# Index logits in pairs of heads, tie operations spread over the attention items, score banks that alternate

## What is computed

```python
# indexer and selected attention (dsa_attention), per block of 128 queries
logits = einsum('bqhd,bsd->bqhs', iq, ik) * 64**-0.5          # 8 index heads, one shared key
score = einsum('bqhs,bqh->bqs', relu(logits), iw * 8**-0.5)
score = where(key_chunk <= query_chunk, score, -inf)
_, idx = top_k(score, 256)                                     # equal scores: the lowest index wins
s = q . k[idx] * 64**-0.5 + t5_table[bucket(idx - qpos)]
out = softmax(s) @ v[idx]
...
# chunk_band_attention: each chunk of 64 sees itself and 8 chunks before it, plus a relative bias
# memory_attention: softmax(q . km * 64**-0.5) @ vm over 256 memory tokens
mixed = concat([ya * silu(a_g), yb * silu(bg), yc * silu(cg), ym * silu(mg)])
y = mixed @ w_out + b_out
```

## Time and profile before

| | |
|---|---|
| three runs | 3225.81, 3226.44, 3231.88 us |
| profiled execution | 3226.48 us, span 3224.7 us |
| busy in the span | PE 2913.3 us (90%), DVE 1745.2 (54%), ACT 874.9 (27%), POOL 634.5 (20%) |
| index logits (TensorE's first to last) | 1204.8 to 1284.7 us |
| remaining rows and channels, counting | to 1557.5 us on PE, 1539.8 on DVE |
| ties | 1540.0 to 1576.7 us |
| attention items | 1561.7 to 1761.8 us |

### The profile page before, as it was taken

One profiled execution on the slowest core, in us unless ns is written; L12 is line 12 of the kernel. 1 busy time (PEld: TensorE's weight loads), 2 busy tenths in 40 slices (PEclk: granted clock), 3 DMA queues, 4 the chain that ended last, 5 costly groups with the idle time before them and its releaser, 6 DMA issues. The chain is left out here.

```text
span 3224.7 us, 34616 instructions
## 1 busy us (share of the span) xinstructions
PE 2913.3 (90%) x13624; PEld 2334.2 (72%) x13624; DVE 1745.2 (54%) x2465; ACT 874.9 (27%) x1262; POOL 634.5 (20%) x298
## 2 busy tenths in 40 slices
PE   6899999999999899999687989955688999998997
PEld 3788888788887684888455768845576888886876
DVE  3699997737256705939767624068763322322032
ACT  2111112234143315121365201134421212222221
POOL 0000000001000010022000024436302434333664
PEclk9999999999999999999799989978898999999999
DMA  6111322233355410111101221100031111112343
GB/s 245 59 53 59 100 77 72 91 123 109 111 163 151 150 48 20 51 46 46 43 1 52 106 69 52 39 0 0 27 122 61 46 52 46 52 46 65 118 131 97
DMA packets 86639, 241.97 MB, mean 75 GB/s; under 512 B 6818, under 2 KB 33826, under 8 KB 84212
## 3 DMA queue, kind: packets, MB, share of 16 engines
q1 hardware_dynamic: 81620, 222.17, 21.0%
q10 hardware_dynamic: 4640, 17.30, 1.4%
q0 software_dynamic: 256, 0.82, 0.1%
HBM read 206.71 MB, written 33.55 MB: 75 GB/s over the span
## 5 line engine op out<-in xcount | busy, mean ns | idle before, releaser
L294 PE MATMUL pair<-u_hi,w_hi 128*128 128x512 f32 x768 | 300.8, 392 | 12.0 <-DVE w_lo L603 11.7
L552 DVE SCALAR_TENSOR_TENSOR conv_acc<-aT,cols,conv_acc 128x1024 f32<-128x1024 f32 x232 | 297.9, 1284 | 6.8
L295 PE MATMUL pair<-u_lo,w_hi 128*128 128x512 f32 x768 | 299.7, 390 | 0.0
L296 PE MATMUL pair<-u_hi,w_lo 128*128 128x512 f32 x768 | 299.6, 390 | 0.0
L294 PE MATMUL pair<-h_hi,up_hi 128*128 128x512 f32 x704 | 275.0, 391 | 7.4 <-POOL up_lo L289 7.4
L295 PE MATMUL pair<-h_lo,up_hi 128*128 128x512 f32 x704 | 274.8, 390 | 0.0
L296 PE MATMUL pair<-h_hi,up_lo 128*128 128x512 f32 x704 | 274.7, 390 | 0.0
L2475 DVE SCALAR_TENSOR_TENSOR ua<-pair,cols,ua 128x1023 f32<-128x1023 f32 x44 | 56.4, 1282 | 340.6 <-ACT ua L2459 340.6
L914 POOL TENSOR_TENSOR yrT<-yrT,gate_c 128x1024 f32<-128x1024 f32 x8 | 19.0, 2371 | 807.7 <-ACT yrT L807 807.7
L294 PEld LDWEIGHTS pair<-u_hi,w_hi 128*128 128x128 f32 x768 | 144.8, 189 | 43.1 <-DVE w_lo L603 12.0
L1695 DVE TENSOR_SCALAR_CACHE_REDUCE counted<-choice,top_i 128x384 uint8<-128x384 f32 (+2 forms) x192 | 168.9, 942 | 0.1
(11 more groups left out here) (387 smaller groups left out, 6501.7 us busy)
## 6 DMA issues: line engine op xcount, KB each, us to landing
wt<-in_w_ch SPq DMA_DIRECT2D x65, 512.0 KB, 3.4
wo_raw<-in_w_out SPq DMA_DIRECT2D x48, 512.0 KB, 3.6
wt<-in_w_up SPq DMA_DIRECT2D x44, 512.0 KB, 3.2
wt<-in_w_down SPq DMA_DIRECT2D x44, 512.0 KB, 3.6
ada<-in_ada_w SPq DMA_DIRECT2D x8, 1536.0 KB, 8.5
wt<-in_w_conv SPq DMA_DIRECT2D x16, 512.0 KB, 3.5
qk<-qk_st SPq DMA_DIRECT2D x8, 1024.0 KB, 6.3
gates<-qk_st ACTq DMA_DIRECT2D x16, 512.0 KB, 2.6
```

The source lines that it names most:

```text
L294: nc.tensor.matmul(bank, w[0], x[0], start=(first and k == 0), stop=False)
L295: nc.tensor.matmul(bank, w[0], x[1], start=False, stop=False)
L296: return nc.tensor.matmul(bank, w[1], x[0], start=False, stop=(last and k == n_k - 1))
L552: nc.vector.scalar_tensor_tensor(dst, x, w, conv_acc[:], ALU.mult, ALU.add).then_inc(conv_step, 1)
```

## The change

Three parts. (1) The logits go by two heads: for each 512 columns the matmul of both heads, the wait is for the relu of the first head of the pair before, and filler steps come only between pairs. (2) The six operations of a tile's ties become 36 single calls of `tie_operation`, one at the end of each of the items 0 to 35 in VectorE's queue; a selected item waits until its tile's six are done; `top_i` and `top_f` move to another place, as the bias buffer lies over the old one, and the bias DMA no longer waits. (3) An item of up to 512 columns uses one bank of each head's pair, bank n % 2, and scores(n) wait for the last item before it that used the same bank; wider items use both.

```diff
--- before.py
+++ after.py
@@ -1364,8 +1364,8 @@
         counted = at(13, "counted", [P, 2, S], mybir.dt.uint8)
         iws = at(205, "iws", [P, TT, 8])
         small3 = at(205.25, "small3", [P, 80])
-        top_i = at(205.625, "top_i", [P, 3, 6], I32)
-        top_f = at(205.75, "top_f", [P, 2, 6])
+        top_i = at(15.5, "top_i", [P, 3, 6], I32)
+        top_f = at(15.625, "top_f", [P, 2, 6])
@@ -1516,17 +1516,19 @@
             pe.wait_ge(ch_out, 5)
             pe.wait_ge(row_ok, TT)
             at_fill = 0
-            for n, (t, g) in enumerate(logits):
-                if n >= 3:
-                    pe.wait_ge(relu_ok, n - 2)
-                r = 64 * (g % 2)
+            for n in range(0, len(logits), 2):
+                t, g = logits[n]
+                if n >= 2:
+                    pe.wait_ge(relu_ok, n - 1)
                 for c0 in range(0, (t + 1) * P, HALF):
                     w = min(HALF, (t + 1) * P - c0)
-                    last = nc.tensor.matmul(pair[n % 3][:, c0 // HALF, 0:w],
-                                            chT[chan("iq", g // 2)][r:r + 64, t * P:(t + 1) * P],
-                                            chT[chan("ik")][r:r + 64, c0:c0 + w], start=True, stop=True)
-                last.then_inc(lg_mm, 1)
-                while at_fill < (n + 1) * 4 * KT // len(logits):
+                    for r in (0, 64):
+                        last = nc.tensor.matmul(pair[(n + r // 64) % 3][:, c0 // HALF, 0:w],
+                                                chT[chan("iq", g // 2)][r:r + 64, t * P:(t + 1) * P],
+                                                chT[chan("ik")][r:r + 64, c0:c0 + w], start=True, stop=True)
+                        if c0 + w == (t + 1) * P:
+                            last.then_inc(lg_mm, 1)
+                while at_fill < (n + 2) * 4 * KT // len(logits):
                     channel_step(pe, FILL[at_fill // (2 * KT)], at_fill % (2 * KT))
                     at_fill += 1
             pe.wait_ge(relu_ok, len(logits))
@@ -1754,25 +1756,25 @@
-            done = 1
-            for t in range(2, TT):
...
-                nc.vector.tensor_scalar(sc, sc, 1.0, -NEG, ALU.subtract, ALU.mult).then_inc(tie_step, 1)
-                done += 6
-            dve.wait_ge(tie_step, done)
-            dve.sem_inc(top_done, 1)
+        def tie_operation(dve, n):
+            t, i = 2 + n // 6, n % 6
+            sc, x = choice[:, SC_AT[t]:SC_AT[t] + (t + 1) * P], tie[:, 0:(t + 1) * P]
+            least, room = top_i[:, 0, t - 2:t - 1].bitcast(F32), top_f[:, 1, t - 2:t - 1]
+            dve.wait_ge(tie_step, n + 1)
+            if i == 0:
                 nc.vector.tensor_scalar(x, sc, least, None, ALU.is_equal).then_inc(tie_step, 1)
+            elif i == 1:
                 nc.vector.tensor_tensor_scan(out=x, data0=ones_col[:].broadcast_to([P, (t + 1) * P]), data1=x, initial=0.0,
                                              op0=ALU.mult, op1=ALU.add).then_inc(tie_step, 1)
+            elif i == 2:
+                nc.vector.tensor_scalar(x, x, room, None, ALU.is_le).then_inc(tie_step, 1)
+            elif i == 3:
                 nc.vector.scalar_tensor_tensor(x, sc, least, x, ALU.is_ge, ALU.mult).then_inc(tie_step, 1)
+            elif i == 4:
                 nc.vector.scalar_tensor_tensor(sc, sc, least, x, ALU.is_gt, ALU.max).then_inc(tie_step, 1)
+            else:
                 nc.vector.tensor_scalar(sc, sc, 1.0, -NEG, ALU.subtract, ALU.mult).then_inc(tie_step, 1)
         bias_b = [at(201, "bias_b0", [P, 2, BAND]), at(46, "bias_b1", [P, 2, BAND])]
@@ -1833,10 +1835,24 @@
         def rep_slot(m):
             return pair[3][:, m % 2, P:2 * P]
 
+        N_TIES = 6 * (TT - 2)
+
+        def score_banks(n):
+            if width(n) > HALF:
+                return (0, 1)
+            return (n % 2,)
+
+        def free_when(n):
+            users = [m for m in range(n) if set(score_banks(m)) & set(score_banks(n))]
+            return users[-1] if users else None
+
+        def score_view(n, hh):
+            b = score_banks(n)
+            return flat(pair[hh])[:, b[0] * HALF:b[0] * HALF + width(n)]
+
         def attend_sync(sp):
             sp.wait_ge(ch_mm, N_CH)
             sp.dma_start(bias_b[1][:], a["bias_b"][:, 2:4, :]).then_inc(at_bias[1], 16)
-            sp.wait_ge(top_done, 1)
             sp.dma_start(bias_b[0][:], a["bias_b"][:, 0:2, :]).then_inc(at_bias[0], 16)
             sp.wait_ge(a_mixed, 2)
             sp.dma_start(t5[:], a["bias_c"]).then_inc(at_c, 16)
@@ -1848,16 +1864,17 @@
             def scores(n):
                 g, t, p = at_items[n]
                 first, _ = g["span"](t)
-                if n:
-                    if at_items[n - 1][0]["bias"]:
-                        pe.wait_ge(drained, biased[n])
+                before = free_when(n)
+                if before is not None:
+                    if at_items[before][0]["bias"]:
+                        pe.wait_ge(drained, biased[before + 1])
                     else:
-                        pe.wait_ge(ex_ok, 2 * n)
+                        pe.wait_ge(ex_ok, 2 * before + 2)
                 for c0 in range(0, width(n), HALF):
                     w = min(HALF, width(n) - c0)
                     for hh in range(2):
                         r = 64 * hh
-                        last = nc.tensor.matmul(pair[hh][:, c0 // HALF, 0:w],
+                        last = nc.tensor.matmul(pair[hh][:, score_banks(n)[c0 // HALF], 0:w],
                                                 chT[g["q"] + p][r:r + 64, t * P:(t + 1) * P],
                                                 g["keys"](2 * p + hh)[:, first * P + c0:first * P + c0 + w],
                                                 start=True, stop=True)
@@ -1907,7 +1924,7 @@
                 act.wait_ge(sc_max, 2 * n + hh + 1)
                 if g["bias"] is None and n >= 2:
                     act.wait_ge(attr_mm, last_unit[n - 2])
-                nc.scalar.activation(s_, s_ if g["bias"] else flat(pair[hh])[:, 0:width(n)], ACT.Exp,
+                nc.scalar.activation(s_, s_ if g["bias"] else score_view(n, hh), ACT.Exp,
                                      bias=nmax[:, n % 2 * 2 + hh:n % 2 * 2 + hh + 1],
                                      accum_out=sums[:, n % 4 * 2 + hh:n % 4 * 2 + hh + 1]).then_inc(ex_ok, 1)
 
@@ -1933,7 +1950,7 @@
             def maxima(n, hh):
                 g, t, p = at_items[n]
                 w, i = width(n), n % 2 * 2 + hh
-                s_, p_, m_ = g["s"][:, i, 0:w], flat(pair[hh])[:, 0:w], mx[:, i:i + 1]
+                s_, p_, m_ = g["s"][:, i, 0:w], score_view(n, hh), mx[:, i:i + 1]
                 dve.wait_ge(atsc_mm, 2 * n + hh + 1)
                 if n >= 2:
                     dve.wait_ge(ex_ok, 2 * (n - 2) + hh + 1)
@@ -1951,6 +1968,7 @@
                     else:
                         nc.vector.tensor_tensor(s_, p_, bias, ALU.add).then_inc(drained, 1)
                         dve.wait_ge(drained, biased[n] + hh + 1)
+                        dve.wait_ge(tie_step, 1 + 6 * (t - 1))
                         nc.vector.tensor_tensor_reduce(out=s_, in0=s_, in1=mask, scale=1.0, scalar=LOWEST,
                                                        op0=ALU.add, op1=ALU.max, accum_out=m_).then_inc(maxed, 1)
                 dve.wait_ge(maxed, 2 * n + hh + 1)
@@ -1995,6 +2013,8 @@
                     maxima(n, 1)
                 if n >= 3:
                     mix(n - 3)
+                if n < N_TIES:
+                    tie_operation(dve, n)
 
         with nc.Block() as block:
             @block.sync
```

More of the change, by code:

```diff
@@ L1402, in build @@
         lg_mm, relu_ok, acc_ok = sem("lg_mm"), sem("relu_ok"), sem("acc_ok")
-        corner_set, counts_ok, step_ok, cand_ok, thr_ok, tie_step, top_done = (sem("top_" + x) for x in (
-            "corner", "counts", "step", "cand", "thr", "tie", "done"))
+        corner_set, counts_ok, step_ok, cand_ok, thr_ok, tie_step = (sem("top_" + x) for x in (
+            "corner", "counts", "step", "cand", "thr", "tie"))
         QB = [chan("bq"), chan("bq", 1), chan("cq"), chan("cq", 1), chan("mq"), chan("mq", 1)] + \
```

8 lines of the change are left out of this document (removed).

## The result

The changed kernel takes **3200.97 us** (median of 4 runs, 3200.19 to 3202.01) where the kernel before takes 3226.12 (4 runs beside it): ratio 0.9921, 95% interval 0.9907 to 0.9935. It is 25.15 us faster; forecast were 17.0. The forecast of 3209.5 is 8.5 us too slow, and its range began at 3204. The direction was right, the size was not.

A forecast was written before the change was run, and what follows sets the result against it. TensorE bounds the stretch between logits and attention; VectorE's ties leave it idle 15.57 us before the attention. 3226.48 less 7.6 (logits) less 9.4 (attention: 17.0 - 5.0 - 2.9 + 0.3) gives 3209.5 us, range 3204 to 3214, with rival 2 to 3217.

The forecast's parts named there:

- the term for the memory items: Attention items 0 to 15: with two banks and ties among them, item 16 starts at 1608.8 instead of 1625.82, +17.0 us.
- First 16 heads and the wait: Logits: the first 16 heads gain 2.2 us; at the mid-logit wait the pair (24, 25) loses 0.3.
- Heads 26 to 47: Logits: one unit fewer in heads 26 to 31, +1.3 us; 8 units instead of 11 in heads 32 to 47, +5.3.
- Counting stretch: Behind the logits: TensorE fills it and VectorE's counting doesn't bind, so the logits' gain reaches its end; 0 of its own.
- With the same lag: Start of the attention: full clock returns 15.6 us after TensorE's restart, as before, so score 5 ends at 1577.5.
- full clock at once: Upper bound of the attention's gain: no low clock turns five items of 3.66 us into 2.6, +4 us.
- Narrow band items: Attention items 16 to 23: VectorE's own 19.4 us and 7.3 of ties exceed the old 21.6, -5.0 us.
- Items 24 to 35: Items 24 to 31 hide ties in VectorE's idle 1.80 us each, 0; the first four selected items run late, -2.9 us.
- the second (logits held by relu and accumulation): Rival: in the last 16 heads TensorE waits for both relus of the pair before; 3216.2 us, 10%.
- the third: Rival: in the attention each tie is added to the loop of score, maximum, exponent; slower, 3236.1 us, 4%.
- fourth: Rival: banks bring nothing in the memory items, wide items hide their ties; no change, 3221.7 us, 5%.
- The first, the low clock through the memory items: Rival: the clock stays at 1.2 GHz until item 16, with items of 3.66 us; 3219.4 us, 8%.

The follow-up runs named there:

- ties_only: The kernel before with the ties moved among the attention items, old logits, every narrow score in bank 0: 3224.07 us, ratio 0.9991.
- banks_only: The kernel before with narrow scores alternating between two banks, old logits, all 36 ties in one block ahead of the attention: 3212.50 us, ratio 0.9954.
- early_scores: The changed kernel with the first two scores ahead of ScalarE's last two evacuations: 3204.04 us, ratio 0.9928.

## Why the prediction was wrong in size

The step that failed is the term for the memory items, +17.0. To item 47 the traces differ by 9.0 us from the forecast, and more than half of that, 4.7 us, lies there. By the steps of the sum, in the two traces:

- **First 16 heads and the wait: +1.9 forecast, +2.2 measured.** Right; the wait became 4.36 us.
- **Heads 26 to 47: +1.3 and +5.3 forecast, 7.8 measured** (the stretch from the wait's end to the last logit's end went from 42.6 to 34.8), of which heads 26 to 31 gave 2.1 and heads 32 to 47 5.7. In the last 16 heads the forecast was right term by term, with 1.07 us of relu waiting in five places for the 1.1 added up; the 0.4 us more are the two places with two filler steps in a row, 1.59 us each and not 2 x 0.90. For heads 26 to 31 a trace says little: the three other traces with the old logits are 1.5 us longer than the one before. The end, -0.9 forecast, measured -0.85.
- **Counting stretch: 0 forecast, 1.1 measured.** Not the change's: from the row projection to the first scores it takes 272.3 to 273.9 us in the traces with the old logits and 272.6 with the new. In the first 58 us of it the clock reads 0.91 before and 0.94 after the change, and 0.94 in *ties_only*, which keeps the old logits and takes 272.3.
- **Memory items: +17.0 forecast, +21.7 measured, the step that failed.** The path was right, VectorE with its ties behind a low clock; two terms were mis-sized. "With the same lag" took the 15.6 us of low clock from a start in which TensorE paused 1.23 us behind its first transposes; the change itself removes that pause, and full clock came after 8.5 us (that the pause is the cause is argued from the table above, not shown by itself). By item 5 this had brought 2.3 us (13.5 us from the first scores, forecast 15.8). And an item with its tie costs 0.2 us less than the sum of the two: the 2.0 us ran to the end of the last operation, but the tie starts 1.92 us after the maximum and the next maximum 0.66 us after a tie of 0.74, while the ties of the block, from which I took their cost, start 0.04 us after each other's ends. From item 5 to 16 it was 29.0 us, not 31.3. My bound for "full clock at once" (+4) stood in the text, but the range's lower end took it or the logits' upper bound, not both, and a part of both came.
- **Narrow band items: -5.0 forecast, -3.95 measured.** As argued, with the same overlap: 6.5 us for the ties and 19.0 for VectorE's own, from start to start, where the sum had 7.3 and 19.4. **Items 24 to 35: 0 and -2.9 forecast, -1.5 and -0.7 measured**: wrong in where, right within 1 us in sum. Item 31, whose tie is the longest (2.28 us), took 5.59 us instead of 4.12, so not every tie fits, and one of the signs of being wrong (over 5 us for a wide item) was met there.
- Behind item 47's sum, where nothing was forecast, the changed kernel's trace loses 2.2 us, 1.5 of them to the low clock at 1728.34, and ahead of the logits 2.5 are gained by the execution.

Of the rivals, the second (logits held by relu and accumulation) is refuted: it needs 3.6 and 4.0 us from a pair over a single step to the next, for both relus, and the trace has 2.77 and 3.10, for one; the third and fourth rested on ties that hide nowhere and banks that bring nothing, and *ties_only* and *banks_only* refute both. The first, the low clock through the memory items, did not come true in the changed kernel but is real: in *early_scores* it lasted to item 6. The Trainium skill, TensorE: Matmul & The Clock Gate, section on the second failure mode (psum-queue depth-cycling), tells of a bf16 kernel with 512 columns whose clock oscillates where TensorE cycles through PSUM banks with small idle times. *banks_only* alternates banks with TensorE busy for 144.63 of 163.00 us and the clock at 1.00 throughout, so banks and small idle times alone don't do it here; the clock fell once, in the changed kernel, behind a stretch where TensorE was idle for 1.6 of 4 us (1591 to 1595).

## What to carry to other kernels

A low clock is part of a stall's price and goes with it: where a change removes a pause behind a restart, cost the start with a short lag and with a long one, and keep both in the range, rather than taking the lag of the old trace. Removing a wait in a loop can bring more than the waits, where fewer rounds then run at the low clock (with the banks two of 3.66 us became 2.07). Look first for the resource with one buffer (here the score bank), since moving the other work (the ties) brings little by itself: beside two banks the traces show nothing of it. And an idle stretch of an engine ahead of a phase (23 us of VectorE here) takes deferred work at no cost, where the same work inside the phase costs what is not hidden.

## What the runs showed that I had not expected

- TensorE's low clock lasted 3.6 to 21 us behind its restart where the attention begins, and up to 16.00 us of it with TensorE busy all the time; the same code had 6.9 and 10 us in different executions.
- Starting a phase earlier made it slower: two pauses of 2.26 and 2.05 us cost 3.6 us more than one of 4.27. Three useless repeats of a matmul in the second pause gave 5.8 us back.
- A filler step of three matmuls with 512 columns takes 0.90 us alone between logits, and 0.80 and 0.79 where two follow one another.
- The shortest waits have no bracket in a timeline: three of the five waits for the relu in the last 16 heads show only in the distance from start to start.
- ScalarE loads a table for 1.28 us between a relu and an evacuation with bias, on TensorE's path.
